# Index query projection of a sparse-attention layer: full-array matmuls split into pairs of 64-row matmuls with separate PSUM banks

## The reference, cut to what matters

```
proj = x @ w_in
q, k, v, iq, ik, iw = jnp.split(proj, A_SPLITS, axis=-1)      # iq: 8 heads x 64
...
iq = partial_rotary(iq.reshape(bsz, L, IDX_HEADS, IDX_DIM), cos, sin)
ik = partial_rotary(ik, cos, sin)
...
s = jnp.einsum('bqhd,bsd->bqhs', iq_b, ik) * IDX_DIM ** -0.5
score = jnp.einsum('bqh,bqhs->bqs', iw_b, jax.nn.relu(s))
_, sel = lax.top_k(score, top_k)
```

## Time and profile before

| | before |
|---|---|
| median of 3 runs | 1239.79 us (1239.36 to 1240.22) |
| profiled execution, its own time | 1238.46 us |
| its span, first to last instruction | 1236.5 us |
| PE busy | 1223.8 us (99% of the span) |
| DVE busy | 853.4 us (69%) |
| ACT busy | 589.3 us (48%) |
| POOL busy | 92.9 us (8%) |
| mean DMA rate | 180 GB/s |

### The profile page before, as it was taken

How to read it: one execution, slowest core, us unless ns; L and a number is a source line. 1 busy time by engine, 2 the same in 40 slices (tenths; PEclk the granted TensorE clock), 3 DMA queues, 4 the chain that set the end, 5 groups by cost and what they waited for, 6 DMA issues and landing times.

```text
span 1236.5 us, 18630 instructions
## 1 busy us (share of the span) xinstructions
PE 1223.8 (99%) x7934; PEld 1044.4 (84%) x7934; DVE 853.4 (69%) x920; ACT 589.3 (48%) x714; POOL 92.9 (8%) x222
## 2 busy tenths in 40 slices
PE   8999999999999999999999999999999999999998
PEld 7888888888888888888988888888898888888887
DVE  6897766665865776666776676667587666666675
ACT  5774444434644544333654444435472544444434
POOL 4631000001000200000101000001000100000000
PEclk9999999999999999999999999999999999999999
DMA  9425656555533755654615655555554247555632
GB/s 334 153 70 171 215 193 196 182 201 156 205 136 123 252 196 183 200 184 147 226 56 188 220 178 197 189 185 205 186 191 154 103 151 242 194 191 183 203 140 100
DMA packets 126818, 222.07 MB, mean 180 GB/s; under 512 B 6000, under 2 KB 90496, under 8 KB 126736
## 3 DMA queue, kind: packets, MB, share of 16 engines
q1 hardware_dynamic: 123840, 210.88, 50.5%
q0 software_dynamic: 2896, 10.01, 2.5%
HBM read 219.82 MB, written 1.05 MB: 179 GB/s over the span
## 4 chain that ended last, share of the span: by engine, by line
PE 92%; DVE 3%; DMA 2%; ACT 2%; issue 1%; POOL 1%; SPq 0%; DVEq 0%; POOLq 0%
PE ps L794 20%; PE ps L622 18%; PE ps L796 10%; PE ps L599 10%; PE ps L600 10%; PE ps L601 10%; PE ps L762 5%; PE ps L706 2%; PE ps L806 2%; DVE wlo L1830 1%; PE ps L970 1%; DMA raw<-in_a_w_in 1%; PE ps L1109 1%; ACT whi L1381 1%; PE ps L918 1%
## 5 line engine op out<-in xcount | busy, mean ns | idle before, releaser
L1830 DVE TENSOR_TENSOR wlo<-raw,whi 128x2048 fp32r<-128x2048 f32 (+3 forms) x204 | 452.2, 2232 | 172.2 <-ACT whi L1381 171.2
L1381 ACT ACTIVATE whi<-raw 128x2048 fp32r<-128x2048 f32 (+3 forms) x204 | 377.0, 1861 | 73.2 <-DMA raw<-in_hgrn_w_in 21.1
L794 PE MATMUL ps<-xhl,whi 128*128 128x512 f32 x1088 | 271.5, 391 | 0.0
L794 PEld LDWEIGHTS ps<-xhl,whi 128*128 128x128 f32 x1088 | 198.5, 188 | 37.5
L622 PE MATMUL ps<-whi,xhl 128*128 128x512 f32 (+2 forms) x736 | 183.9, 382 | 1.2 <-ACT xhl L1398 0.6
L599 PE MATMUL ps<-whi,hh 128*128 128x512 f32 x432 | 168.9, 391 | 0.0
L600 PE MATMUL ps<-whi,hl 128*128 128x512 f32 x432 | 168.6, 390 | 0.0
L601 PE MATMUL ps<-wlo,hh 128*128 128x512 f32 x432 | 168.1, 389 | 0.0
L796 PEld LDWEIGHTS ps<-xhl,wlo 128*128 128x128 f32 x1088 | 148.4, 190 | 10.6
L622 PEld LDWEIGHTS ps<-whi,xhl 128*128 128x128 f32 x736 | 131.6, 188 | 27.1 <-DVE wlo L1830 1.2
L796 PE MATMUL ps<-xhl,wlo 128*128 128x256 f32 x1088 | 151.7, 282 | 0.0
(11 more groups left out here) (329 smaller groups left out, 1338.2 us busy)
## 6 DMA issues: line engine op xcount, KB each, us to landing
raw<-in_ffn_w_in SPq DMA_DIRECT2D x40, 1024.0 KB, 5.0
raw<-in_mlp_w_up SPq DMA_DIRECT2D x32, 1024.0 KB, 5.3
raw<-in_mlp_w_down SPq DMA_DIRECT2D x32, 1024.0 KB, 4.9
raw<-in_ffn_w_down SPq DMA_DIRECT2D x22, 1024.0 KB, 4.8
raw<-in_hgrn_w_in SPq DMA_DIRECT2D x16, 1024.0 KB, 5.5
raw<-in_b_w_in SPq DMA_DIRECT2D x12, 1024.0 KB, 5.2
raw<-in_ple_w_gate SPq DMA_DIRECT2D x8, 1024.0 KB, 5.8
raw<-in_a_w_in SPq DMA_DIRECT2D x5, 1024.0 KB, 6.1
```

What stands on the lines that cost most here:

```text
L794: mm(bank(b + f), w[0][:, kk, P * f : P * f + P], xhl[:, kk, :, :].rearrange("p a n -> p (a n)"), start=(kk == 0), stop=False)
L1381: a.activation(whi[:, slot, 0:w], raw[:, slot, 0:w], ACT.Copy).then_inc(s["hi_done"], 1)
L1830: v.tensor_tensor(wlo[:, slot, 0:w], raw[:, slot, 0:w], whi[:, slot, 0:w].bitcast(F32), ALU.subtract).then_inc(s["lo_done"], 1)
```

## The change

Each 128-row matmul of the index queries becomes two matmuls over 64 rows: the upper half of the contraction piece (rows 0 to 63) accumulates into bank `tt`, the lower half (rows 64 to 127) into bank 2 + `tt`. The two partial sums have to be added, so ScalarE now copies the upper half sums of both tiles, and VectorE adds the lower half sums to what ScalarE wrote, in place.

```diff
@@ GpSimd
-            pool.wait_ge(s["iq_act"], 1)
-            pool.wait_ge(s["iq_dve"], 1)
+            pool.wait_ge(s["iq_dve"], 2)
@@ TensorE, index_queries
                         for tt in range(TT):
-                            last = mm(bank(2 + tt), (xh, xl)[part][:, k0 + kk, P * tt : P * tt + P], w[w_part][:, kk, :],
-                                      start=(k0 + kk == 0 and (part, w_part) == (0, 0)), stop=(k0 + kk == KD - 1 and w_part == 1))
+                            for e, own in enumerate(parts_of(64)):
+                                last = mm(bank(2 * e + tt), (xh, xl)[part][own, k0 + kk, P * tt : P * tt + P], w[w_part][own, kk, :],
+                                          start=(k0 + kk == 0 and (part, w_part) == (0, 0)), stop=(k0 + kk == KD - 1 and w_part == 1))
@@ TensorE, before dsa_q 0
-            pe.wait_ge(s["iq_act"], 1)
-            pe.wait_ge(s["iq_dve"], 1)
+            pe.wait_ge(s["iq_act"], 2)
+            pe.wait_ge(s["iq_dve"], 2)
@@ ScalarE
             act.wait_ge(s["w_done"], first["dsa_iq"] + len(IQ_PARTS))
-            a.activation(kvi[:, 0, 512:1024], bank(2), ACT.Copy).then_inc(s["iq_act"], 1)
+            for tt in range(TT):
+                a.activation(kvi[:, tt, 512:1024], bank(tt), ACT.Copy).then_inc(s["iq_act"], 1)
             until(first["dsa_q"])
@@ VectorE
             dve.wait_ge(s["w_done"], first["dsa_iq"] + len(IQ_PARTS))
-            v.tensor_copy(kvi[:, 1, 512:1024], bank(3)).then_inc(s["iq_dve"], 1)
+            for tt in range(TT):
+                dve.wait_ge(s["iq_act"], tt + 1)
+                v.tensor_tensor(kvi[:, tt, 512:1024], bank(2 + tt), kvi[:, tt, 512:1024], ALU.add).then_inc(s["iq_dve"], 1)
             until(first["dsa_keys"] + 1)
```

## The result

| | before | after |
|---|---|---|
| median | 1239.50 us (1239.03 to 1240.94, 9 runs) | 1243.18 us (1241.70 to 1245.04, 9 runs) |
| ratio, 95% interval | | 1.0028 (1.0019 to 1.0037) |
| profiled execution, its span | 1236.5 us | 1241.1 us |

The change makes the kernel slower by 0.28%, 3.5 us. The time lies in the range of the prediction, but more than twice as far from the start as the forecast of 1.6 us.

What follows compares the result with a forecast made beforehand. VectorE was taken to bound the stretch before the second key chunk: 0 for matmuls, 0 for changes of form, +1.6 us through VectorE, so 1241.4 us against the median of 1239.79; range 1239.6 to 1244.5 us.

Steps and rivals of the forecast that it cites:

- The price of a pair: Index products on TensorE: two 64-row halves run side by side, costing 0.227 us, the same as one full matmul.
- The rival in which the halves take turns: Index products: the two halves of a split matmul do not overlap; +7.8 us, 1247.6 us, chance 0.07.
- weight loads that are not hidden: Index products: a split matmul costs 0.33 us because its loads show; +3.1 us, 1242.9 us, chance 0.07.
- The path through VectorE: Before the second key chunk: VectorE waits 0.94 us for ScalarE, then one more instruction; 1.54 to 1.65 us, taken as 1.6.
- Nothing later is tied to absolute time: Behind the second key chunk: all later work moves by the same 1.6 us, with nothing added or taken back.
- the hole of 1.8 us: TensorE before the second key chunk: idle from 23.3 to 25.1 us, waiting for VectorE's remainder.
- the rival in which the delay grows on its way: Behind TensorE's new idle: lower clock, or GpSimd or a load adds 1 us or more; 1242.4 to 1244.5 us, chance 0.06.
- GpSimd's alignment: GpSimd's rotation before the transposes: its first instruction ends with VectorE's remainder, so it moves 1.6 us, as TensorE does.

Runs made afterwards that it cites:

- The pairs alone with the hole filled: Kernel before with only the split matmuls, copies as before, plus 18 transposes behind the second index chunk; 1239.72 us, ratio 0.9995.
- The copies alone: Kernel before with only the change's copies and additions, the index products staying 48 full-array matmuls; 1242.65 us, ratio 1.0020.
- filling the hole: Kernel before with only the change's copies and additions, plus 14 unused transposes between the two key chunks; 1240.78 us, ratio 1.0006.
- the same 96 instructions without pairs: Kernel before with 24 tiny 32x16 matmul calls added behind the second index chunk; 1241.29 us, ratio 1.0007.
- The moved additions: Changed kernel with VectorE's two additions moved behind the remainder of the second key chunk; 1247.33 us, ratio 1.0054.
- 40 tiny calls: Changed kernel with 40 tiny 32x16 matmul calls added behind the second index chunk; 1241.40 us, ratio 1.0016.

## Why the prediction was right and where it was not

- **The price of a pair** (0.227 us) was right: eight pairs in 1.82 us. The rival in which the halves take turns and the one of weight loads that are not hidden are both out. The pairs alone with the hole filled stand at a ratio of 0.9995. The row used for it was misread in one point: a plain float32 matmul is recorded as two, so the eight matmuls of the earlier trace rows are four calls, two pairs. The price of one recorded matmul, 0.216 us, and the conclusion stay.
- **The path through VectorE** was right step by step: new wait 1.02 us (0.94 forecast), two additions in 1.29 us, remainder at 23.52, TensorE's second key chunk at 25.09 (25.1), delay 1.57 us (1.6).
- **"Nothing later is tied to absolute time, so the sum is" +1.6** is the step that failed. It held for the waits between engines, and left out two things. The first is the clock. The forecast saw the hole of 1.8 us and set a falling clock aside, because a hole of 2.2 us had left the clock at 1.00 in the earlier trace rows. That row covers the wait itself, and there the changed kernel reads 1.00 too; a fall shows behind the wait. Nor could the digits of the earlier trace rows show one, since 3.4 us at half the clock in a slice of 31 us leave some 94%, still a 9. The stretch behind the wait was indeed at 1.00 before, but that is one execution, and it was taken for a rule. The copies alone show the fall in the profiled execution and, by their two groups of times, in some seven of ten; filling the hole takes 0.14% away. This was the rival in which the delay grows on its way, with its price of 1 to 3 us about right and its chance of 0.06 too low.
- The second thing left out is **the count of TensorE instructions**. 96 more brought stops of 2.5 us in all at 330 and 950 us, in matmuls that the change does not touch. Nothing in the prediction speaks of it. That TensorE waits there for its next instructions is shown by the table above: ten pauses in six kernels at the same three places of the list, a multiple of 256 apart, each ending 1.3 to 1.6 us after a block had landed. The shift decides which instructions stand at these places. How long a pause gets hangs on how early the block is fetched: the same 96 instructions without pairs brought only 0.5 us in the profile.
- **GpSimd's alignment** was counted right: its first instruction ended at 23.79 + 1.56 = 25.35, 0.3 us after VectorE's remainder as before, and TensorE did not wait for it. The moved additions show how near that was.
- The forecast of 1.6 us, 0.13%, was too small, and the change can be told from none: 0.28% with an interval from 0.19 to 0.37. That 1243.18 us lies inside the range is in part luck: its top, 1244.5, took in weight loads that are not hidden, which did not occur, and stops of which nobody had thought filled the room. The three parts are about 1.6 us (delay), up to 1.7 us (clock behind a hole) and up to 2.5 us (stops). They do not simply add, since in the profiled execution the fall of the clock was hidden behind the delay.

Open is how often each of the two falls of the clock happens in the changed kernel and how long the stops are in its other executions, since only one execution of each kernel is profiled. Open is also why a hole of 1.9 us was followed by a fall and one of 2.1 us was not.

## What to carry to other kernels

Splitting a full-array matmul into two halves over 64 rows gains nothing on TensorE and needs an addition afterwards; ask first where that addition stands in the list of the engine that is waited for. A new hole of 2 us on TensorE can cost nearly its length twice, once as delay and once through the clock behind it, and useless matmuls in the hole took the second part back. To see such a fall, read the granted clock of the 5 us behind a hole, not in it. Where a change alters the number of TensorE instructions, look in the profile of after for idle time put down to issue in dense short matmuls, however far away, and count the instructions up to it: the same count in two kernels points at the fetching of the list.

## What the runs showed of the hardware that was not expected

- After holes of about 2 us the granted clock fell in some profiled executions and not in others: it stayed at 1.00 after the hole of 2.13 us in the kernel before and after that of 2.12 us with 40 tiny calls, and was 0.50 from 26.3 to 29.7 us after a hole of 1.9 us in the copies alone.
- TensorE stopped for 1.8 us within 64 short matmuls and for 3.12 us some 3 us behind 160 of them, with no engine to wait for. Such pauses stood at places 449, 4289 and 12737 of its recorded list in six kernels, a multiple of 256 apart, and ended 1.3 to 1.6 us after a 16 KB transfer of the instruction queue.
- A GpSimd instruction of 0.22 us took 2.27 us when a VectorE subtraction of 2048 columns between two SBUF operands was under way.
- A plain float32 matmul is recorded as two matmuls with two weight loads: 48 calls appeared as 96.
